# Regrouping the panels around four norms and reordering the reloads of a two-layer Hyena/MLA/FNet step on one core

## What is computed

```python
def trunk_layer(h, ada, l, P, ...):
    n = rmsnorm(h, norm_g[l, 0]) * (1 + sc0) + s0
    h = h + 0.5 * g0 * swiglu(n, w_ffn_up[l, 0], w_ffn_down[l, 0])      # D_FF = 2816
    n = rmsnorm(h, norm_g[l, 1]) * (1 + sc1) + s1
    proj = n @ w_in[l]                         # hyena 768, q 256, kv 128, rope 32, fnet 256, gates 3*1024
    y_a = hyena_mixer(...) @ w_hy_out[l]       # long convolution by transforms
    y_b = blocked_attention(q, k, v) @ w_mla_o[l]   # 8 heads, latent keys and cached context keys
    y_c = real(fft2(fn)) @ w_fnet[l]
    g_a, g_b, g_c = split(sigmoid(gates), 3)
    y = (g_a * y_a + g_b * y_b + g_c * y_c) @ w_out[l]
    h = h + g1 * y
    n = rmsnorm(h, norm_g[l, 2]) * (1 + sc2) + s2
    return h + 0.5 * g2 * swiglu(n, w_ffn_up[l, 1], w_ffn_down[l, 1])
```

## Time and profile before

| | us |
|---|---|
| median of three runs | 3584.61 |
| the profiled execution, own time | 3590.41 |
| its span | 3588.6 |
| TensorE busy | 3219.9 (90%) |
| VectorE busy | 1893.9 (53%) |
| ScalarE busy | 1002.6 (28%) |
| mean granted TensorE clock | 0.948 |

### The profile page before, as it was taken

The page is one execution under the profiler, slowest core; times in us unless marked ns, Lnnn a source line. Parts: engine busy times, 40 slices in busy tenths (PEclk is TensorE's granted clock), DMA queues, the critical chain, the costliest instruction groups (busy, mean ns, idle before and its releaser), DMA issues.

```text
span 3588.6 us, 47627 instructions
## 1 busy us (share of the span) xinstructions
PE 3219.9 (90%) x20308; PEld 3076.7 (86%) x20308; DVE 1893.9 (53%) x3092; ACT 1002.6 (28%) x1500; POOL 155.1 (4%) x156
## 2 busy tenths in 40 slices
PE   2999999677999799999999999987689988999998
PEld 2999999446888789999989999884478877999998
DVE  7546565567544455344455555646765545553234
ACT  2212123223333323121232222321233333321222
POOL 0000000221000000000000000011300000000000
PEclk9999999778999899999999999997789998999999
DMA  5333334113112422222322333241131134232221
GB/s 220 128 119 142 140 118 162 62 47 126 72 67 84 183 101 95 100 106 86 109 95 107 150 126 138 92 174 38 70 135 67 63 125 153 80 120 71 83 71 65
DMA packets 67651, 384.99 MB, mean 107 GB/s; under 512 B 7856, under 2 KB 10224, under 8 KB 40048
## 3 DMA queue, kind: packets, MB, share of 16 engines
q1 hardware_dynamic: 54432, 297.82, 22.6%
q10 hardware_dynamic: 5712, 47.42, 3.2%
q0 software_dynamic: 7296, 36.70, 2.7%
HBM read 340.33 MB, written 41.58 MB: 106 GB/s over the span
## 4 chain that ended last, share of the span: by engine, by line
PE 71%; DVE 15%; ACT 6%; DMA 5%; issue 3%; ACTq 0%; DVEq 0%; SPq 0%; POOL 0%; POOLq 0%
PE tile_psum L468 34%; PE tile_psum L475 17%; PE tile_psum L710 4%; PE tile_psum L429 3%; PE misc_psum L665 3%; PE tile_psum L397 3%; ACT whi L919 2%; DVE wlo L1291 2%; PE misc_psum L397 2%; PE tile_psum L714 2%; PE tile_psum L434 1%; DMA raw<-in_w_gate 1%; DVE scaled L1343 1%; PE misc_psum L629 1%; DVE n_lo L1360 1%
## 5 line engine op out<-in xcount | busy, mean ns | idle before, releaser
L468 PE MATMUL tile_psum<-n_hi,whi 128*128 128x320 f32 x3200 | 741.1, 313 | 31.6 <-DVE n_lo L1360 25.4
L468 PE MATMUL tile_psum<-n_lo,whi 128*128 128x320 f32 x3200 | 735.7, 311 | 0.0
L468 PEld LDWEIGHTS tile_psum<-n_hi,whi 128*128 128x128 f32 x3200 | 539.5, 190 | 41.9 <-DVE n_lo L1360 30.8
L468 PEld LDWEIGHTS tile_psum<-n_lo,whi 128*128 128x128 f32 x3200 | 541.8, 190 | 0.0
L1291 DVE TENSOR_TENSOR wlo<-raw,whi 128x2048 fp32r<-128x2048 f32 (+2 forms) x196 | 431.0, 2199 | 199.1 <-ACT whi L919 197.7
L475 PE MATMUL tile_psum<-n_hi,wlo 128*128 128x320 f32 x3200 | 512.5, 313 | 0.0
L919 ACT ACTIVATE whi<-raw 128x2048 fp32r<-128x2048 f32 (+1 forms) x216 | 397.0, 1838 | 393.1 <-DMA raw<-in_w_up 195.7
L475 PEld LDWEIGHTS tile_psum<-n_hi,wlo 128*128 128x128 f32 x3200 | 487.5, 192 | 0.0
L468 PE MATMUL tile_psum<-x_hi,whi 128*128 128x320 f32 x1408 | 323.2, 310 | 5.2 <-DVE h L1436 5.2
L468 PE MATMUL tile_psum<-x_lo,whi 128*128 128x320 f32 x1408 | 322.2, 310 | 0.0
L1468 DVE TENSOR_TENSOR hidden<-gate_act,tile_psum 128x320 f32<-128x320 f32 x176 | 85.5, 486 | 395.0 <-ACT gate_act L998 394.6
(11 more groups left out here) (269 smaller groups left out, 4129.4 us busy)
## 6 DMA issues: line engine op xcount, KB each, us to landing
raw<-in_w_up SPq DMA_DIRECT2D x88, 1024.0 KB, 4.9
w_ada<-in_w_ada SPq DMA_DIRECT2D x128, 512.0 KB, 5.6
raw<-in_w_down SPq DMA_DIRECT2D x32, 1024.0 KB, 4.8
raw<-in_w_gate SPq DMA_DIRECT2D x24, 1024.0 KB, 5.1
raw<-in_tables SPq DMA_DIRECT2D x20, 1024.0 KB, 4.8
g_keep<-gate_out POOLq DMA_DIRECT2D x48, 320.0 KB, 2.6
gates<-g_keep POOLq DMA_DIRECT2D x16, 960.0 KB, 6.7
raw<-in_w_down SPq DMA_DIRECT2D x16, 768.0 KB, 4.3
```

What stands on the lines that cost most here:

```text
L468: pe.matmul(tps[:, t.s, m, 0:TH], blk(p, m * n + k)[0], (hi, lo)[b][:, k, tok], start=k == 0 and b == 0, stop=False)
```

## The change

- **Norms.** Three panels instead of two go A A A B B B: `walk(last=True)` ends (1,0), (2,0), (3,0), (1,1), (2,1), (3,1) after (0,0), (0,1), and `walk(first=True)` begins (0,0), (1,0), (2,0), (0,1), (1,1), (2,1). The sums of half 0 stand within step (1,1), its spread after it; the sums of half 1 after the next stage's step (0,0), the spread within (1,0). Eight blocks of the norm are written as 0 to 3 and 4 to 7 after two different steps. The last section before a norm is a function of its own (`into_h_last`), written out step by step. Two `ada` tiles move from the last down section of FFN0 to an earlier one.
- **Mix.** Columns are laid out anew, so that the first three panels (fnet, hyena 0 to 255, q) go as three pairs; panels 3 to 5 follow in one piece each.
- **Heads.** Seven F pieces lead; the F pieces behind Q(0), Q(1), T(0) and P(0) to P(3) are gone. R is split into R (ScalarE's round) and L (VectorE's split), two items later, and R is kept out of the stretch from T(5n+3) to P(n).
- **Proj.** Three gate buffers instead of two. On GpSimd's queue x blocks 6, 7 and gate 1 move ahead of the last `g_keep` write; x blocks 0, 1 wait for the heads' end and the last `g_keep` write, and no longer for `h`; `h` moves from ScalarE's queue to GpSimd's, behind gate 3.

```diff
-ADA_PLAN = [[0, 0, 2, 2, 1, 1, 1, 1] + [1] * 4 + [2] * 8 + [1] * 4 + [2] * 6 + [2, 2, 0, 0],
+ADA_PLAN = [[0, 0, 2, 2, 1, 1, 1, 1] + [1] * 4 + [2] * 8 + [2, 2, 1, 1] + [2] * 6 + [1, 1, 0, 0],
...
     if first:
-        steps[:4] = [(0, 0), (1, 0), (0, 1), (1, 1)]
+        steps[:6] = [(i, j) for j in range(2) for i in range(3)]
     if last:
-        steps[-4:] = [(n - 2, 0), (n - 1, 0), (n - 2, 1), (n - 1, 1)]
+        steps[-6:] = [(i, j) for j in range(2) for i in range(n - 3, n)]
...
-    order = []
+    order = [("F", 0)] * 7
...
-                    order += [("Q", hd), ("F", 0), ("K", hd), ("QS", hd)]
+                    order += [("Q", hd)] + [("F", 0)] * (hd > 1) + [("K", hd), ("QS", hd)]
...
-            order += [("T", n - 2), ("F", 0)]
+            order += [("T", n - 2)] + [("F", 0)] * (n != 2)
             if n % 5 == 1:
-                order += [("P", (n - 2) // 5), ("F", 0)]
+                order += [("P", (n - 2) // 5)] + [("F", 0)] * (n not in (6, 11, 16, 21))
...
+        for a, b in busy:
+            if a <= last < b:
+                last = b
...
+        rounds.setdefault(min(last, len(order) - 1), []).append(panel)
+        splits.setdefault(min(last + 2, len(order) - 1), []).append(panel)
...
-                for i, j in steps[:4]:
-                    late = (i, j) == (0, 0) and not opened
-                    pair(i, j, n, hi, lo, coming(j) if i == 0 else None, (lambda: token_sums(1)) if late else None)
-                    if late:
-                        spread(1)
+                for i, j in steps[:6]:
+                    late = (i, j) == (1, 0) and not opened
+                    pair(i, j, n, hi, lo, coming(j) if i == 0 else None, (lambda: spread(1)) if late else None)
+                    if (i, j) == (0, 0) and not opened:
+                        token_sums(1)
...
                         if c == 3 * KT - 4:
                             pool.wait_ge(q_split, 1 + HEADS * (l + 1))
                             gates_kept(0)
                             pool.dma_start(gb[:, 0], g_keep[0]).then_inc(g_in[0], 16)
-                    pool.wait_ge(prob_in, 5 * HEADS * (l + 1))
-                    for hl, x_ in enumerate((xh, xl)):
-                        pool.dma_start(x_[:, 6:8, :].bitcast(F32), x_keep[hl][:, 2:4]).then_inc(x_back[1], 16)
-                    gates_kept(1)
-                    pool.dma_start(gb[:, 1], g_keep[1]).then_inc(g_in[1], 16)
+                        if c == 3 * KT - 1:
+                            pool.wait_ge(prob_in, 5 * HEADS * (l + 1))
+                            for hl, x_ in enumerate((xh, xl)):
+                                pool.dma_start(x_[:, 6:8, :].bitcast(F32), x_keep[hl][:, 2:4]).then_inc(x_back[1], 16)
+                            gates_kept(1)
+                            pool.dma_start(gb[:, 1], g_keep[1]).then_inc(g_in[1], 16)
+                        pool.wait_ge(fill_free, 48 * l + 2 * c + 2)
+                        pool.dma_start(g_keep[c // 3, :, c % 3, :], gate_out[c % 3][:, :]).then_inc(g_kept[c % 3], 16)
+                    pool.wait_ge(heads_done, l + 1)
                     gates_kept(KT - 1)
-                    pool.wait_ge(h_back, 16 * (l + 1))
                     for hl, x_ in enumerate((xh, xl)):
                         pool.dma_start(x_[:, 0:2, :].bitcast(F32), x_keep[hl][:, 0:2]).then_inc(x_back[0], 16)
                     for m in range(2, KT):
-                        pool.wait_ge(y_used, l * KT + m - 1)
-                        pool.dma_start(gb[:, m % 2], g_keep[m]).then_inc(g_in[m % 2], 16)
+                        if m > 2:
+                            pool.wait_ge(y_used, l * KT + m - 2)
+                        pool.dma_start(gb[:, m % 3], g_keep[m]).then_inc(g_in[m % 3], 16)
+                        if m == 3:
+                            pool.dma_start(h[:, :, :], h_keep).then_inc(h_back, 16)
...
-                act.wait_ge(spilled, due.now(spilled))
-                act.dma_start(h[:, :, :], h_keep).then_inc(h_back, 16)
...
+                if layer < DEPTH:
+                    normalise(layer, norm, 0, m0, range(4))
+                else:
+                    finish(0, m0)
```

More of the change, by code:

```diff
@@ L138, in head_order @@
             done[n * 4] = at
-    turns, last = {}, 0
+        elif what == "P":
+            busy.append((order.index(("T", 5 * n + 3)), at))
+    rounds, splits, last = {}, {}, 0
     for panel in range(2, 18):
         last = max(last, done.get(panel - 3, -2) + ROUND_LAG)
-        assert last < first.get(panel, len(order))
-        turns.setdefault(min(last, len(order) - 1), []).append(panel)
+        for a, b in busy:
+            if a <= last < b:
+                last = b
+        assert last + 3 < first.get(panel, len(order) + 9)
+        rounds.setdefault(min(last, len(order) - 1), []).append(panel)
+        splits.setdefault(min(last + 2, len(order) - 1), []).append(panel)
     fills = 0
@@ L147, in head_order @@
         fills += what == "F"
-        out += [("R", panel) for panel in turns.get(at, [])]
+        out += [("R", panel) for panel in rounds.get(at, [])] + [("L", panel) for panel in splits.get(at, [])]
     assert fills == 2 * 2 * 24
@@ L990, in ffn, with into_h, into_h_last @@
-            def ffn(f, norm, last):
+                due(sq_used)
+            def into_h():
+                for i, j in walk(4):
+                    slots.tile()
+                    if j == 0:
+                        round_panel()
+            def into_h_last(layer, i):
+                squares_of(0, 0)
+                round_panel()
+                squares_of(0, 1)
+                squares_of(1, 0)
+                round_panel()
+                squares_of(2, 0)
+                squares_of(3, 0)
+                token_root(0)
+                squares_of(1, 1)
+                if layer < DEPTH:
+                    norm_hi(layer, i, 0, range(4))
+                    round_panel()
+                squares_of(2, 1)
+                if layer < DEPTH:
+                    norm_hi(layer, i, 0, range(4, KT))
+                    round_panel()
+                squares_of(3, 1)
+                token_root(1)
@@ L991, in ffn @@
+            def ffn(norm, last):
                 for c, n in enumerate(CHUNKS):
                     for i, j in walk(n, first=c == 0):
-                        first = c == 0 and (i, j) == (0, 0)
-                        if first:
-                            norm_hi(*norm, 1, range(4))
                         t = tile()
@@ L1444, in into_h @@
+            def into_h(section, plan):
+                for i, j in walk(4):
+                    update(section, i, j)
+                    if j == 0:
                         split_panel()
                         ada_step(plan[i])
-                    if last and (i, j) == (3, 0):
-                        m0 = open_norm(0)
-                    if last and (i, j) == (2, 1) and last[0] < DEPTH:
-                        normalise(*last, 0, m0, range(5))
-                    if last and (i, j) == (3, 1) and last[0] < DEPTH:
-                        normalise(*last, 0, m0, range(5, KT))
-                        m1 = open_norm(1)
-                        split_panel()
-                        return m1
@@ L1455, in into_h, with into_h_last @@
-                    if last and (i, j) == (2, 1) and last[0] == DEPTH:
-                        finish(0, m0)
+            def into_h_last(section, plan, layer, norm):
+                update(section, 0, 0)
+                split_panel()
+                ada_step(plan[0])
+                sum_squares(0, 0)
+                update(section, 0, 1)
+                sum_squares(0, 1)
+                update(section, 1, 0)
+                split_panel()
+                ada_step(plan[1])
+                sum_squares(1, 0)
+                update(section, 2, 0)
+                sum_squares(2, 0)
+                update(section, 3, 0)
+                sum_squares(3, 0)
+                m0 = open_norm(0)
+                update(section, 1, 1)
+                if layer < DEPTH:
+                    normalise(layer, norm, 0, m0, range(4))
+                else:
+                    finish(0, m0)
+                sum_squares(1, 1)
+                update(section, 2, 1)
+                if layer < DEPTH:
+                    normalise(layer, norm, 0, m0, range(4, KT))
+                    split_panel()
+                sum_squares(2, 1)
+                update(section, 3, 1)
+                sum_squares(3, 1)
+                if layer < DEPTH:
+                    split_panel()
+                return open_norm(1)
@@ L1461, in ffn @@
                     for i, j in walk(n, first=c == 0):
-                        first = c == 0 and (i, j) == (0, 0)
-                        if first:
-                            normalise(*norm, 1, m1, range(4))
                         t = tile()
```

184 lines of the change are left out of this document (90 added, 94 removed).

## The result

The changed kernel takes 3475.2 us (median of four runs from 3471.95 to 3479.7); its ratio to the kernel before is 0.9692, with a 95% interval from 0.9676 to 0.9709. It is faster by 110 us; the prediction said 104 and 3481. The profiled execution took 3474.05 us with a span of 3472.2, that is 116.4 less than the span before, since the profiled execution of before lay above its median.

What follows compares the result with a forecast made beforehand. TensorE was taken as the bound, with gains only from its idle stretches or clock. Norms 41, proj 46 and heads 17 sum to 104 us off the profiled 3590.4; the median, 5.8 lower, gives 3481, range 3446 to 3522.

Steps and rivals of the forecast that it cites:

- proj: Proj stage: earlier x and gate loads and three gate buffers leave 9.0 of 31.9 us lost; gain 23 a layer, 46.
- FFN0 to mix: FFN0's last down section into mix: losses of 16.9 and 20.0 us become 11.7; gains of 5 and 8.
- heads: Heads stage: waits fall from 23.3 to 17.3 us, clock gives 2.5; gain 8.5 a layer, 17.
- out to FFN1: Out into FFN1's first up panels: norm blocks come ahead of their readers, 0.5 of 10.0 us loss stays; gain 19.
- FFN1 to FFN0: FFN1's last down section into FFN0: loss falls from 13.7 to 5.7 us, waits for sums staying; gain 8.
- the end: Last FFN1: `finish(0)` stands two steps earlier, so the update of (3,1) is not held up; gain 1 us.
- The new wait for mix panel 3: Mix: load of 15.2 us beside the spill plus rounding of 1.84 makes TensorE wait 3.0 us.
- The two waits for the sums: FFN0 to mix: a wait of some 1.9 inside step (1,1) and another behind (0,0), 4.0 us together.
- the rival on queues: Proj and mix: second x pair 2 us later, gate 4 late behind `h`, panel 3 slower; 28 us less gained, 3509; chance 0.20.
- cleaner: Heads and mix: waits at start and last P vanish, panel 3 loads in time; 20 and 9 us more, 3452; chance 0.15.
- The leading pieces did not fill the wait for `qn_lo`: Heads' start: rival that leading pieces do fill the 12.5 us wait, 2 x 12.3 us more gained, 3456; chance 0.03.
- The slower case: Heads, proj and norms: 28 short waits each followed by low clock, 143 us lost, 3624; chance 0.03.

Runs made afterwards that it cites:

- the late spill: Changed kernel with the spill of `n_keep` and `h_keep` issued behind the rounding of mix panel 3, not before its load: 3469.11 us, ratio 0.9679.
- the kernel with four leading pieces: Changed kernel with low_split wait moved, x's high half early, `h` last, spill late, and four leading gate pieces instead of seven: 3456.39 us, ratio 0.9645.
- the rounds alone: Kernel before with only the heads' rounds and splits set apart and rounds kept out of T to P, gate pieces as before: 3544.87 us, ratio 0.9894.

## Why the prediction was right, step by step

The forecast was 104 and the profiled spans differ by 116; the terms were off by more than the sum, and their errors partly cancel: proj gave 12 less than forecast, FFN0 to mix 12 and heads 8 more. So the mechanisms were for the most part right, and that the sum came this near is in part luck.

| term | predicted | measured | 
|---|---|---|
| FFN0 to mix, both layers | 13 | 9.0 + 15.6 = 24.6 |
| out to FFN1, both layers | 19 | 10.1 + 10.8 = 20.9 |
| FFN1 to FFN0 | 8 | 10.1 |
| the end | 1 | 1.4 |
| proj, both layers | 46 | 15.8 + 18.3 = 34.1 |
| heads, both layers | 17 | 25 (12.9 in layer 0) |

**FFN0 to mix: mechanism right, sizes off.** The new wait for mix panel 3 came as worked out: 3.0 predicted, 2.54 and 1.66 measured, under loads of 14.6 and 13.7 where the earlier trace rows had 15.2, and the late spill took it away. The two waits for the sums, 4.0 in the prediction, are 1.38 and 0.21 in layer 0, 1.16 and 1.01 in layer 1. TensorE in time, layer 0:

```profile
529.59 0.80 PE L489 MATMUL misc_psum<-constants,sq_sum 128*128 128x2 f32 x6 [1.38 <-DVEq L1452]
552.30 0.80 PE L489 MATMUL misc_psum<-constants,sq_sum 128*128 128x2 f32 x6 [0.21 <-DVEq L1452]
591.62 0.56 PE L433 MATMUL tile_psum<-n_hi,whi 128*128 128x320 f32 x2 [2.54 <-ACT whi L926]
```

Two terms were mis-sized, by about the same. The prediction left 11.7 us a layer: 7.0 of waits and 4.7 of clock, the latter by the row of a wait of 3.70. At its pace of 146.6 ns the 866 long matmuls of the wider windows and the norm need 129.9, so 7.6 and 4.1 us are left (an estimate): 4.1 and 3.8 of waits, and 3.5 and 0.3 of clock and small gaps, at a granted clock of 0.98 and 1.00. The waits are now 2.5 and less, so they lie between the row with 1.61, which left the clock at 1.00, and the one with 3.70.

On the Trainium skill's page "DMA: Bandwidth & Descriptors", section "Queues, rings and completion order", the estimate for this load was 11 to 12.5 us. That estimate took 300 to 330 GB/s; the traces show 372 from 576 to 606 us before the change and 398 from 576 to 592 us after it, which would make the estimate 9 to 10. Measured are 14.6 beside the spill and 4.8 without it: the two queues do share the engines, and the panel got less than this estimate gave it.

**Out to FFN1, FFN1 to FFN0, the end.** As predicted, within some 2 us each.

**Proj: the step that failed is the landing of the last write, and behind it the split of a panel.** The gain fell short by 12 us in two layers: the wait for x has some 5 of them, the waits for `mixed` 4 and the clock and small gaps 3. The landing of the last write was taken as 2.6 to 3.5 us after its issue; it took 5.2. This write in the kernel before, then in the changed one (KB, us to landing), and GpSimd of the changed kernel in time, the last write and the x pair behind it:

```profile
g_keep<-gate_out POOLq DMA_DIRECT2D x1, 320.0 KB, 11.2
```

```profile
g_keep<-gate_out POOLq DMA_DIRECT2D x1, 320.0 KB, 5.2
...
1171.16 0.55 POOL L900 DMA_DIRECT2D g_keep<-gate_out  x1 [9.07 <-ACT gate_out L1240]
1176.96 0.54 POOL L904 DMA_DIRECT2D x_hi<-x_keep  x1 [5.25 <-DMA g_keep<-gate_out]
```

The 2.6 was the median of 48 writes; this one took 11.2 before, beside `h`, a proj panel and the loads issued just behind it, and the change took `h` away from it but not the panel, issued at 1170.4, just ahead of it. In layer 1, behind a panel too, it took 5.5. That the panel is what holds it up is read from these times; in the kernel with four leading pieces, where the panel is issued 5.2 us ahead of the write, the write takes 3.4, but no run moves the panel alone. The pair then took 5.7, near the 5.8 that the prediction gave it, and TensorE waited 6.09 and 6.42 instead of 3.8, just past the far end of the stated bounds (3 to 6). Loading half of the pair earlier cut this to 5.0 in each layer. The second part: `h` was weighed against gate 4, which came in time; it was the proj panel that `h` delayed, to 10.3 us, and the split of that panel stands on VectorE ahead of the products of the fourth output block. VectorE in time, then TensorE:

```profile
1206.17 2.29 DVE L1316 TENSOR_TENSOR wlo<-raw,whi 128x2048 fp32r<-128x2048 f32 x1 [3.32 <-ACT whi L926]
...
1209.99 0.57 PE L433 MATMUL tile_psum<-x_hi,whi 128*128 128x320 f32 x2 [3.76 <-DVE mixed L1822]
```

The wait of 3.76 there and the clock behind it are what the rival on queues had priced at 6 and 5, with another transfer as the victim; moving `h` took 4 us of it back. The other part of the term held: gate waits are gone, blocks wait 0.3 to 0.4 elsewhere in layer 0 (layer 1 keeps one of 2.31). The prediction took x's wait of 11.2 as a sign that `h` and x share the engines; it isn't one, since the second pair waited for `h` by a semaphore. The panel's 10.3 beside `h` and 4.7 without it is.

**Heads: the sum of the waits was near, by parts that were not.** The list of waits came to 15.7 in layer 0 (17.3 predicted), with 2.99 at P(3) (2.5), 0.43 at P(1) (2.0) and none at the two others (0.4 each); the gain in clock and small gaps, 5 us, was larger than the 2.5 that I took. That the wait for `qn_lo` stays because `low_split` stands ahead of the pieces is shown by the changed kernel (12.75) and by the edit that moves it. What the prediction did not see is that the leading pieces take some 15 us from what the rounds alone give. It had counted their missing fillers, 5.8 at the start, and a wait of 2.5 at P(3), but not that this wait comes from the split which the pieces push in there, nor the clock behind it.

**The rivals.** The condition of "cleaner" did not come: panel 3's load still made TensorE wait (2.54 and 1.66), and heads kept waits at the start and at P(3); that mix and heads gave 20 us more than forecast came from the sizes above. "Queues" is half true for proj: the second pair landed some 2 us later and a transfer was late behind `h`, but the panel and not gate 4. The leading pieces did not fill the wait for `qn_lo`, as the order's row said; with the wait moved behind them they filled part of it (16.7 us in two layers). The slower case fell: in heads of layer 0 eight waits of 0.8 to 1.7, beside one of 2.05 and one of 2.99, leave the granted clock at 0.98.

## What to carry to other kernels

A stage's floor by the undisturbed pace, and the waits by name above it, gave the sum within about a tenth, partly because errors cancelled; what was least sure was the clock behind a wait, for which rows of several lengths on both sides of the wait are wanted. The time a transfer takes is to be read from the row of that transfer in its place: the median of 48 writes hid the one of 11.2 us that mattered. After a change that moves transfers, look for the transfer that was not moved and now shares the time with them (here a weight panel, not the gates). A list of items with rules for some of them has to be read again after each edit: a piece moved at the front put a split in front of a product of the fourth head, and taking the parts of a change one by one showed that one of them cost what another gave.

## What the runs showed of the chip

A 1 MB panel took 14.6 us to land beside a spill of 7.5 MB and 4.8 without it, 10.3 beside the 2.5 MB of `h` and 4.7 without it; a write of 320 KB issued 0.7 us behind a panel took 5.2 where 2.6 is usual, and 11.2 beside a panel, `h`, a pair of x and a gate. The granted clock stayed at 1.00 over 134 us with waits of 1.16, 1.01 and 1.66 in them.
